# Half of the last down product's K as a 2 by 2 block product in seven products

## What is computed

```python
D_MODEL, SEQ, D_FF_2 = 2048, 256, 8192
...
    return x + jnp.square(jax.nn.relu(h @ w_up)) @ w_down     # w_up [2048, 8192], w_down [8192, 2048]
...
# then: out = rms_norm_2(x, ln_f_w)  = x * rsqrt(mean(x*x) + eps) * ln_f_w
```

## Time and profile before

| | us |
|---|---|
| median of 3 runs | 2757.39 |
| lowest, highest | 2757.25, 2757.7 |
| span of the profiled execution | 2755.5 |
| `down2_b`: first matmul to end of the last | 2573.70 to 2747.80 = 174.10 |
| behind the last matmul | 2747.80 to 2755.5 = 7.7 |

### The profile page before, as it was taken

One profiled execution on the slowest core, in us unless ns is written; L12 is line 12 of the kernel. 1 busy time (PEld: TensorE's weight loads), 2 busy tenths in 40 slices (PEclk: granted clock), 3 DMA queues, 4 the chain that ended last, 5 costly groups with the idle time before them and its releaser, 6 DMA issues.

```text
span 2755.5 us, 37706 instructions
## 1 busy us (share of the span) xinstructions
PE 2740.9 (99%) x15082; PEld 2323.4 (84%) x15082; DVE 1712.7 (62%) x2348; ACT 1343.8 (49%) x1966; POOL 54.1 (2%) x99
## 2 busy tenths in 40 slices
PE   9999999999999999999999999999999999999998
PEld 7888888888888888888888888888888888888887
DVE  5666676666664676665666687557656654466554
ACT  5465555644443444455655475445454343344343
POOL 1001000000000000000100000000000000000000
PEclk9999999999999999999999999999999999999999
DMA  8545455455555655556664445347555565555553
GB/s 334 190 156 204 176 172 184 164 191 196 185 168 192 217 186 187 172 184 212 258 227 148 151 150 195 138 154 279 178 187 189 185 212 191 191 192 190 187 195 137
DMA packets 78721, 523.65 MB, mean 190 GB/s; under 512 B 9688, under 2 KB 9920, under 8 KB 24032
## 3 DMA queue, kind: packets, MB, share of 16 engines
q1 hardware_dynamic: 71552, 489.83, 51.5%
q0 software_dynamic: 7008, 31.56, 3.1%
HBM read 512.94 MB, written 12.35 MB: 191 GB/s over the span
## 4 chain that ended last, share of the span: by engine, by line
PE 96%; DVE 2%; ACT 1%; issue 0%; DVEq 0%; DMA 0%; ACTq 0%; SPq 0%
PE acc L332 19%; PE acc L333 19%; PE acc L338 19%; PE wk L431 15%; PE wk L439 8%; PE acc L431 5%; PE acc L439 2%; PE wk L993 1%; PE wk L963 1%; PE wk L687 1%; PE wk L815 1%; DVE w_lo L231 0%; ACT w_hi L225 0%; PE wk L977 0%; PE wk L1653 0%
## 5 line engine op out<-in xcount | busy, mean ns | idle before, releaser
L231 DVE TENSOR_TENSOR w_lo<-w_raw,w_hi 128x1024 fp32r<-128x1024 f32 (+1 forms) x966 | 1089.8, 1170 | 778.3 <-ACT w_hi L225 776.0
L225 ACT ACTIVATE w_hi<-w_raw 128x1024 fp32r<-128x1024 f32 (+1 forms) x966 | 930.3, 1011 | 1091.9 <-PE acc L338 657.5
L332 PE MATMUL acc<-w_hi,h 128*128 128x512 f32 x1112 | 447.5, 402 | 0.4 <-DVE x L2167 0.3
L431 PE MATMUL wk<-h,w_hi 128*128 128x512 f32 x1824 | 444.8, 391 | 0.0
L333 PE MATMUL acc<-w_hi,h 128*128 128x512 f32 x1112 | 434.2, 390 | 0.0
L431 PEld LDWEIGHTS wk<-h,w_hi 128*128 128x128 f32 x1824 | 335.1, 188 | 64.8
L332 PE MATMUL acc<-w_hi,f_hi 128*128 128x512 f32 x856 | 333.3, 389 | 0.0
L333 PE MATMUL acc<-w_hi,f_lo 128*128 128x512 f32 x856 | 333.1, 389 | 0.0
L338 PE MATMUL acc<-w_lo,h 128*128 128x512 f32 x1112 | 298.4, 390 | 0.0
L338 PEld LDWEIGHTS acc<-w_lo,h 128*128 128x128 f32 x1112 | 208.3, 188 | 45.3 <-DVE w_lo L231 1.7
L332 PEld LDWEIGHTS acc<-w_hi,h 128*128 128x128 f32 x1112 | 208.9, 188 | 44.4 <-issue 1.2
(11 more groups left out here) (473 smaller groups left out, 2482.9 us busy)
## 6 DMA issues: line engine op xcount, KB each, us to landing
w_raw<-in_w_up_a SPq DMA_DIRECT2D x76, 1024.0 KB, 4.9
w_raw<-in_w_up_b SPq DMA_DIRECT2D x72, 1024.0 KB, 4.9
w_raw<-in_w_win SPq DMA_DIRECT2D x59, 1024.0 KB, 4.9
w_raw<-in_w_merge SPq DMA_DIRECT2D x32, 1024.0 KB, 5.0
w_raw<-in_w_down_a SPq DMA_DIRECT2D x32, 1024.0 KB, 4.9
w_raw<-in_w_down_b SPq DMA_DIRECT2D x32, 1024.0 KB, 4.9
w_raw<-in_w_win2g SPq DMA_DIRECT2D x24, 1024.0 KB, 4.9
w_raw<-in_w_down_a SPq DMA_DIRECT2D x24, 768.0 KB, 4.3
```

What stands on the lines that cost most here:

```text
L225: act_.activation(w_hi[:, s % SPL, a:b], w_raw[:, s % RAW, a:b], ACT.Copy).then_inc(hi_ready, 1)
L231: dve_.tensor_tensor(w_lo[:, s % SPL, a:b], w_raw[:, s % RAW, a:b], w_hi[:, s % SPL, a:b].bitcast(F32), ALU.subtract).then_inc(lo_ready, 1)
L332: pe_.matmul(o, self.tile(hi, kt, t), wh, start=kt == 0, stop=False)
L431: pe_.matmul(self.sets[n % 2][m][:, 0:2 * S], w_hi[:, s, c:c + P], h[:, kt0 + k, :, :].rearrange("p a b -> p (a b)"), start=kt0 + k == 0, ...
```

## The change

`down2_b` becomes the class `Seven`. Its K of 32 tiles is halved. Tiles 16 to 31 are done as before: 16 items called W, with K block 4 to 7, 24 matmuls each. Tiles 0 to 15 are done in two groups (g = 0, 1) of 8 tiles. In a group, and for each of two panels (p = 0, 1) of 1024 columns, the product is one of 2 by 2 blocks: the left blocks are 128 tokens x 4 K tiles, the weight blocks are items. It is made from seven products of one left block with one weight block, 12 matmuls each, instead of eight: P1, P2, Q3, Q4, Q5, P6 and P7. That is 28 product items and 16 W items, 44 in all, where there were 32. `ORDER` writes out their sequence as (panel, kind, group or K block, column chunk); k is the place in it, from 0 to 43.

Four of the seven take a sum of weight blocks. In a slot of raw weights, P1's block is loaded, then another block is added to it by an accumulating DMA from POOL for Q5, a third for P6, a fourth for Q4; likewise Q3's block, and one more for P7. An add waits until VectorE has split what stood there. There are 16 such adds of 1 MB and 28 plain loads by SP. One more slot, `w_more`, is there. The four mixed left blocks of each group are made by VectorE in `up2_b` (`mixed`), and split at the start of `down2_b` (`mixed_act`, `mixed_dve`), into `h`, which is free then.

The results lie in eight PSUM banks and are put together by VectorE (`take_first`, `take_plain`, `take_sums`, `take_left`, `take_last`), with waits between steps that depend on each other. The gain is loaded within the stage by POOL, between the adds of both panels. The final norm's steps are spread anew; the last chain of row tile 0 now follows W's last item (k = 42) and that of row tile 1 the last product (k = 43). The scaling by VectorE covers columns 1024 to 2047 in one instruction of 1024, with the gain; before it was 512 with and 512 without the gain.

```diff
+            ORDER = ([(0, "W", 4, 0), (0, "W", 4, 1), (0, "W", 5, 0), (0, "W", 5, 1),
+                      (0, "P1", 0), (0, "W", 6, 0), (0, "Q3", 0), (0, "Q5", 0), (0, "W", 6, 1), (0, "P7", 0),
+                      (0, "P6", 0), (0, "P2", 0), (0, "P1", 1), (0, "W", 7, 0), (0, "Q4", 0), (0, "Q3", 1),
+                      (0, "Q5", 1), (0, "W", 7, 1), (0, "P7", 1), (0, "P6", 1), (0, "P2", 1), (1, "W", 4, 1),
+                      (0, "Q4", 1), (1, "W", 5, 1)]
+                     + [(1, "P1", 0), (1, "W", 4, 0), (1, "Q3", 0), (1, "Q5", 0), (1, "W", 5, 0), (1, "P7", 0),
+                        (1, "P6", 0), (1, "P2", 0), (1, "W", 6, 1), (1, "Q4", 0), (1, "P1", 1), (1, "W", 6, 0),
+                        (1, "Q3", 1), (1, "Q5", 1), (1, "W", 7, 1), (1, "P7", 1), (1, "P6", 1), (1, "P2", 1),
+                        (1, "W", 7, 0), (1, "Q4", 1)])
...
+            LOADED = {"P1": (0, 0), "P2": (1, 0), "Q3": (1, 1)}
+            ADDED = {"Q5": (0, 1), "P6": (1, 1), "Q4": (1, 0), "P7": (0, 1)}
...
+                    s = (self.WHERE[k] if kind in ("W", "P2") else 2 if kind in ("Q3", "P7") else (3, 4)[what[2]])
...
+            def load(self, e):
+                for k, what in enumerate(self.ORDER):
+                    kind = what[1]
+                    if kind in self.ADDED:
+                        continue
...
+                    if self.before[k] is not None:
+                        e.wait_ge(lo_ready, (self.before[k] + 1) * 2)
+                    e.dma_start(self.raw[self.at[k]], self.w[n]).then_inc(self.ready[self.at[k], False], 16)
+
+            def add(self, e):
+                for k, what in enumerate(self.ORDER):
+                    if k == 24:
+                        e.wait_ge(turned_lo, self.turned + 4 * GROUPS)
+                        load(e, "norm_final", row_out[:], t_in["ln_f"].to_broadcast([P, D]))
+                    if what[1] in self.ADDED:
+                        e.wait_ge(lo_ready, (self.before[k] + 1) * 2)
+                        e.dma_start(self.raw[self.at[k]], self.w[self.source(what, self.ADDED[what[1]])],
+                                    accum_op=ALU.add).then_inc(self.ready[self.at[k], True], 16)
...
+                        for c in range(4):
+                            if t == 0 and c == 2:
+                                e.wait_ge(hi_ready, i * 2 + 2)
+                            wh = w_hi[:, s, c * CH:(c + 1) * CH]
+                            pe_.matmul(o[:], hi[:, c, :], wh, start=opens and c == 0, stop=False)
+                            pe_.matmul(o[:], lo[:, c, :], wh, start=False, stop=False)
+                        if t == 0:
+                            e.wait_ge(lo_ready, i * 2 + 2)
+                        for c in range(4):
+                            mm = pe_.matmul(o[:], hi[:, c, :], w_lo[:, s, c * CH:(c + 1) * CH], start=False,
+                                            stop=closes and c == 3)
...
+                    if k == 27:
+                        act_.activation(st[:, 110:111], eps_c, ACT.Sqrt)
+                        e.wait_ge(y_ready, 1)
+                        for t in range(TT):
+                            ins = act_.activation((sq_flat, sums_flat)[t], x[:, t, 0:BY_ACT], ACT.Square, accum_out=self.col(t, 0))
...
+            def take_sums(self, e, p, k):
+                v, v2 = sums_flat[:, 0:CH], sums_flat[:, CH:2 * CH]
+                self.item_finished(e, k)
+                dve_.tensor_tensor(v, self.bank["P6"][:], v2, ALU.subtract).then_inc(evac[0], 1)
+                e.drain()
+                dve_.tensor_tensor(v2, v, self.bank["Q5"][:], ALU.add).then_inc(evac[0], 1)
+                e.drain()
+                ins = self.onto_x(0, 2 * p + 1, v2)
...
+                dve_.tensor_tensor(v2, v2, self.bank["P7"][:], ALU.subtract)
+                dve_.tensor_tensor(v, self.bank["P7"][:], v, ALU.subtract).then_inc(evac[0], 1)
+                e.drain()
+                ins = self.onto_x(1, 2 * p + 1, v2)
...
+                self.onto_x(1, 2 * p, v)
+                e.drain()
...
+            def dve(self, e):
+                for k in range(1, self.N):
+                    self.low(e, k)
...
+                    if k == 19:
+                        self.take_plain(e, 0, 17)
+                    if k == 21:
+                        self.take_sums(e, 0, 19)
+                    if k == 22:
+                        self.take_left(e, 0, 20)
...
+                    if k == 40:
+                        self.take_plain(e, 1, 38)
+                    if k == 42:
+                        self.take_sums(e, 1, 40)
+                self.take_left(e, 1, 42)
+                self.end_sum(e, 0)
+                self.take_last(e, 1, 43)
+                self.end_row(e, 0)
+                self.end_sum(e, 1)
+                self.end_row(e, 1)
```

More of the change, by code:

```diff
@@ L111, in build @@
         at_end = {k: sem(f"{k}_stage") for k in ("act", "dve")}
-        landed = {}
+        pool_landed = [sem(f"pool_landed{i}") for i in range(3)]
+        landed = {f"gates{i}": pool_landed[i] for i in range(3)}
         out_done = sem("out_done")
@@ L3233, in build @@
         ar2.close()
+        GROUPS = 2
         class Squares:
@@ L3261, in dve, with mixed @@
                                        self.f_hi[:, 4 * n:4 * n + 4, :].bitcast(F32), ALU.subtract).then_inc(ep_lo, 1)
+                    if self.gemm.name == "up2_b" and n < 2 * GROUPS:
+                        self.mixed(e, n // 2, n % 2)
+            def mixed(self, e, g, second):
+                one, two = self.sq[:, :, 0:P], self.sq[:, :, P:S]
+                diff, back = mix_raw[:, 2 * g, :, :], mix_raw[:, 2 * g + 1, :, :]
+                if not second:
+                    dve_.tensor_tensor(diff, one, two, ALU.subtract)
+                    e.drain()
+                    return
+                a21_hi, a21_lo, s1, s4 = [f[:, 8 * g:8 * g + 4, P:S] for f in (f_hi, f_lo, f_hi_raw, f_lo_raw)]
+                dve_.tensor_tensor(back, diff, two, ALU.add)
+                dve_.tensor_tensor(s1, a21_hi.bitcast(F32), two, ALU.subtract)
+                e.drain()
+                dve_.tensor_tensor(s1, s1, a21_lo.bitcast(F32), ALU.add)
+                e.drain()
+                dve_.tensor_tensor(s4, one, back, ALU.subtract)
+                e.drain()
         inv2 = st[:, 112:112 + TT]
@@ L3288, in build @@
         arf = ExitStack()
+        f_hi_at = nc.sbuf_base
         f_hi = sb("f2_hi", [P, 32, S], F32R, arf)
+        f_lo_at = nc.sbuf_base
         f_lo = sb("f2_lo", [P, 32, S], F32R, arf)
@@ L3292, in build @@
         sq = sb("sq2", [P, 4, S], F32, arf)
-        flhs = (f_hi, f_lo)
[L3294 to L3304, removed]
@@ L3305, in build @@
-        last = Along(down2, None, sq[:].rearrange("p a b -> p (a b)"), row_out, turns_=False)
-        down2.by_tile = True
+        w_more = sb("w_more", [P, ITEM], F32, arf)
+        row_out_at = nc.sbuf_base
+        row_out = sb("row_out", [P, D], F32, arf)
+        f_hi_raw = nc.alloc_sbuf_tensor_at("f2_hi_raw", [P, 32, S], F32, offset=f_hi_at)
+        f_lo_raw = nc.alloc_sbuf_tensor_at("f2_lo_raw", [P, 32, S], F32, offset=f_lo_at)
+        mix_raw = nc.alloc_sbuf_tensor_at("mix_raw", [P, 2 * GROUPS, 4, P], F32, offset=row_out_at)
@@ L3307, in build @@
+        flhs = (f_hi, f_lo)
+        y_ready = sem("rows_final")
+        more_ready = sem("raw_ready_more")
         left_done, right_done = sem("out_left"), sem("out_right")
         y_sq, y_sum, y_root, y_inv = [sem("out_" + n) for n in ("squared", "summed", "root", "inverse")]
[L3309 to L3350, removed]
@@ new lines, in build @@
+        sums_flat = sums[:].rearrange("p a b -> p (a b)")
+        sq_flat = sq[:].rearrange("p a b -> p (a b)")
+        up2_a = up_squares("up2_a", True)
+        down2_a = down("down2_a", up2_a, 4)
+        down2_a.ed = add_scaled
+        up2_a.hand_epilogue_to(down2_a)
+        stages.append(down2_a)
+        up2_b = up_squares("up2_b", False)
+        down2_b = Seven("down2_b", up2_b)
+        up2_b.hand_epilogue_to(down2_b)
+        out_norm = Norm()
+        stages.append(down2_b)
+        pool_steps.append(down2_b.add)
```

201 lines of the change are left out of this document (198 added, 3 removed).

## The result

The changed kernel takes **2776.43 us** (median of five runs, 2774.45 to 2777.18) where the kernel before takes 2757.38 on the same chip (2757.25 to 2757.70). The ratio is 1.0068, with a 95% interval of 1.0057 to 1.0079: 0.7% slower. The time lies in the stated range of 2752 to 2785, which holds two of the rivals too, but it is 17.9 us above the forecast (2758.5, own range 2754 to 2762). It is what the second rival gave, late adds with the clock: 2775 to 2779.

The account below looks back on a forecast made before the run. TensorE was taken to bound the kernel: -10.9 us for 48 fewer matmuls, +5.1 for VectorE's and ScalarE's stalls, +2.5 tail, +4.4 adds give +1.1, so 2758.5 us; range 2752 to 2785, the forecast's own 2754 to 2762.

Parts of the forecast that it names:

- two of the rivals: Last stage: adds hidden, 2754.1 us, chance 0.20; adds late, with the clock, 2775 to 2779, chance 0.41.
- the second rival: Last stage: adds cost two loads or more and come late, +16.1 us plus clock drops, 2775 to 2779; chance 0.41.
- a count of one's own: Adds in the last stage: each put at 1.5 loads of work by counting megabytes read and written, +4.4 us.

Follow-up runs that it names:

- half-size version: Against the kernel before: one group of the block product instead of two, 8 adds, last two W items by row tile; 2752.23 us, ratio 0.9981.
- order with more room: Changed kernel with items reordered so each add has at least 11 us, and `take_sums` split in two; 2756.81 us, ratio 0.9998 to the kernel before.
- narrow loads: Changed kernel with all adds, but SP's loads bring 256 of 2048 columns except in slot 4; 2763.04 us, ratio 1.0017 to the kernel before.
- plain loads: Changed kernel with its 16 adds issued as plain loads, same queue and waits, sums left out; 2754.22 us, ratio 0.9986 to the kernel before.

## What to carry to other kernels

Fewer matmuls are worth their beat (0.2267 us each here) only as far as what feeds them has room, and a sum made by the DMA engines is paid as two loads: count the engine time of everything in flight in the stretch before each use, other adds included, not the mean share over the stage. Where a resource goes from half to four fifths busy, half the saving without its price can be more than the whole: here the half-size version is 0.2% faster than the kernel before, and the full one 0.7% slower as it was written, level in the order with more room. For a cost that no row shows, take the nearest row rather than a count of one's own.

## What the runs showed of the hardware

- An accumulating DMA of 1 MB takes 7.9 us to land alone and 8.1 with little beside it, a plain load from the same queue 5.1. Back to back it takes 4.87 us against a load's 2.47, and the engines move 178 to 187 GB/s against 360.
- Its issue takes POOL 0.85 us, that of a plain load 0.55.
- In the stage of the change, gaps of TensorE of 4.3 and 2.95 us were each followed by some 4 to 6 us at the 1.2 GHz level, at 2.6 and 2.9 us of cost; so was one of 2.79 in the version with narrow loads, and one of 2.72 in the kernel before, where the clock fell about 1 us behind the gap and for some 3 us. Gaps of 2.43 (the change) and 2.64 (more room) had no such stretch behind them.
- The runs of the versions with 16 adds differ by 2.7 us in five, and by 4.1 and 5.4 in some ten; those with plain loads or one group by 2.4 to 3.1 in seven to eleven, and the kernel before by 2.7 in 22 and 3.5 in 21.
